# Moving the on-chip arena of matmul operands from 384 to 192 modulo 512 bytes

## What is computed

```python
for l in range(DEPTH):                                   # DEPTH = 1
    mod = (cond @ w_ada[l] + b_ada[l]).reshape(b_, N_SUB, 3, d)
    h = modulate(rms_norm(x, norm_gains[l, 0]), mod[:, 0, 0], mod[:, 0, 1])
    x = x + 0.5 * mod[:, 0, 2][:, None, :] * swiglu(h, ffn1_w_in[l], ffn1_w_down[l])
    h = modulate(rms_norm(x, norm_gains[l, 1]), mod[:, 1, 0], mod[:, 1, 1])
    proj = h @ w_in_mix[l]
...
    merged = (jax.nn.sigmoid(r_hg) * (y_hg @ w_up_hg[l])
              + jax.nn.sigmoid(r_gla) * (y_gla @ w_up_gla[l]))
    x = x + mod[:, 1, 2][:, None, :] * (merged @ w_out[l])
    h = modulate(rms_norm(x, norm_gains[l, 2]), mod[:, 2, 0], mod[:, 2, 1])
    x = x + 0.5 * mod[:, 2, 2][:, None, :] * swiglu(h, ffn2_w_in[l], ffn2_w_down[l])
return rms_norm(x, final_norm)
```

## Time and profile before

| | |
|---|---|
| median of 3 executions | 1189.76 us (1188.7 to 1189.96) |
| the profiled execution, its own time | 1188.77 us |
| its span, first to last instruction | 1186.9 us |
| TensorE busy | 1158.7 us, 98% |
| VectorE busy | 781.7 us, 66% |
| ScalarE busy | 507.5 us, 43% |
| GpSimd busy | 90.7 us, 8% |
| mean granted TensorE clock | 0.992 of full |

### The profile page before, as it was taken

How to read it: one execution, slowest core, us unless ns; L and a number is a source line. 1 busy time by engine, 2 the same in 40 slices (tenths; PEclk the granted TensorE clock), 3 DMA queues, 4 the chain that set the end, 5 groups by cost and what they waited for, 6 DMA issues and landing times.

```text
span 1186.9 us, 18541 instructions
## 1 busy us (share of the span) xinstructions
PE 1158.7 (98%) x7385; PEld 1039.3 (88%) x7385; DVE 781.7 (66%) x1061; ACT 507.5 (43%) x646; POOL 90.7 (8%) x137
## 2 busy tenths in 40 slices
PE   5999999999999999999999999999999999999997
PEld 5789999998889997877887888888999999998887
DVE  5788888767777677566463446755868887863222
ACT  6455554452222466555344322234455544452322
POOL 2000000002220122222010001000000000000000
PEclk8899999999999999999999999999999999999999
DMA  9433333337885131122221457442223333332211
GB/s 353 147 104 108 106 106 106 106 97 264 306 288 179 37 102 44 36 71 72 71 72 36 142 178 245 145 142 72 72 71 107 106 106 106 106 97 98 98 63 71
DMA packets 115126, 143.51 MB, mean 121 GB/s; under 512 B 4084, under 2 KB 102784, under 8 KB 115072
## 3 DMA queue, kind: packets, MB, share of 16 engines
q1 hardware_dynamic: 106800, 113.32, 29.2%
q0 software_dynamic: 8064, 29.36, 7.0%
q10 hardware_dynamic: 208, 0.08, 0.0%
HBM read 140.65 MB, written 2.10 MB: 120 GB/s over the span
## 4 chain that ended last, share of the span: by engine, by line
PE 87%; DVE 7%; ACT 4%; issue 1%; DMA 1%; SPq 0%; DVEq 0%; ACTq 0%
PE PS L819 29%; PE PS L575 16%; PE PS L577 15%; PE PS L576 15%; PE PS L898 1%; PE PS L934 1%; PE PS L620 1%; PE PS L904 1%; PE PS L621 1%; PE PS L622 1%; PE PS L733 1%; DVE ACC L1751 1%; DMA ADA<-in_w_ada_dram 1%; DVE ACC0a L1762 1%; ACT WH L1127 1%
## 5 line engine op out<-in xcount | busy, mean ns | idle before, releaser
L1649 DVE TENSOR_TENSOR WL<-RAW,WH 128x2048 fp32r<-128x2048 f32 (+2 forms) x55 | 120.5, 2191 | 129.4 <-ACT WH L1127 129.3
L575 PE MATMUL PS<-HH,WH 128*128 128x512 f32 (+2 forms) x488 | 186.1, 381 | 4.4 <-DVE HL L1677 3.0
L1127 ACT ACTIVATE WH<-RAW 128x2048 fp32r<-128x2048 f32 (+2 forms) x55 | 100.5, 1828 | 194.3 <-PE PS L577 187.7
L577 PE MATMUL PS<-HH,WL 128*128 128x512 f32 (+2 forms) x488 | 177.8, 364 | 0.0
L576 PE MATMUL PS<-HL,WH 128*128 128x512 f32 (+2 forms) x488 | 177.7, 364 | 0.0
L819 PE MATMUL PS<-HH,WH 128*128 128x256 f32 x576 | 163.3, 284 | 0.3
L819 PE MATMUL PS<-HL,WH 128*128 128x256 f32 x576 | 163.0, 283 | 0.0
L819 PE MATMUL PS<-HH,WL 128*128 128x256 f32 x576 | 163.0, 283 | 0.0
L575 PE MATMUL PS<-UH,WH 128*128 128x512 f32 (+1 forms) x416 | 147.0, 353 | 0.0
L577 PE MATMUL PS<-UH,WL 128*128 128x512 f32 (+1 forms) x416 | 145.8, 351 | 0.0
L576 PE MATMUL PS<-UL,WH 128*128 128x512 f32 (+1 forms) x416 | 145.8, 350 | 0.0
(11 more groups left out here) (320 smaller groups left out, 2244.3 us busy)
## 6 DMA issues: line engine op xcount, KB each, us to landing
RAW<-in_ffn_w_in_dram SPq DMA_DIRECT2D x42, 1024.0 KB, 5.1
ADAW<-in_w_ada_dram POOLq DMA_DIRECT2D x56, 512.0 KB, 5.6
RAW<-in_w_in_mix_dram SPq DMA_DIRECT2D x22, 1024.0 KB, 5.3
RAW<-in_ffn_w_down_dram SPq DMA_DIRECT2D x16, 1024.0 KB, 5.1
ADA<-in_w_ada_dram SPq DMA_DIRECT2D x16, 512.0 KB, 10.5
RAW<-in_ffn_w_down_dram SPq DMA_DIRECT2D x7, 768.0 KB, 4.5
RAW<-in_w_out_dram SPq DMA_DIRECT2D x3, 1024.0 KB, 5.1
XST<-in_x_dram SPq DMA_DIRECT2D x4, 512.0 KB, 5.3
```

Source lines behind the costliest of these rows:

```text
L575: mm(ps, whi, ahi, start=start, stop=False)
L577: return mm(ps, wlo, ahi, start=False, stop=stop)
L1127: A(WH[slot(n)][:, 0:size], RAW[slot(n)][:, 0:size], ACT.Copy).then_inc(unit_hi, 1)
L1649: V.tensor_tensor(WL[s][:, 0:size], RAW[s][:, 0:size], WH[s][:, 0:size].bitcast(F32), ALU.subtract)\
```

## The change

`MASKF` goes from a tensor of its own to an offset in the arena (86016), and the arena grows by 448 bytes, so that its content can begin anywhere in a window of 512 bytes. `arena_offset` then takes the first address at 192 modulo 512. The tensor `arena` now begins at 89472 (384 modulo 512, since `MASKF`'s 512 bytes are gone below it), and 320 bytes further, at 89792 = 175 x 512 + 192, its content. All that lies in the arena has moved by 192 bytes down. `RAW`, `WH`, `WL`, `X` stay where they were; the small tensors that came after `MASKF` have moved by a whole 512 bytes. Because `MASKF` now shares its bytes with rows that the feed-forward writes later, VectorE waits for the 27 steps of GpSimd ahead of its first product of gate and up values.

```diff
-        MASKF = sb("MASKF", [P, P])
...
-        arena = sb("arena", [P, (ARENA + 2 * H_BYTES) // 4])
+        arena = sb("arena", [P, (ARENA + 2 * H_BYTES) // 4 + 112])
...
+        MASKF = place("MASKF", [P, P], 86016)
...
+                if which == 0:
+                    dve.wait_ge(consts, 11 + 4 * len(LEVELS))
                 up_times_gate(which, 0, PS[:, 2:4, :], SG[:, :, :])
...
     size = arena.shape[1] * 4
-    return (nc.sbuf_base - size) // 32 * 32
+    start = (nc.sbuf_base - size) // 32 * 32
+    return start + (192 - start) % 512
```

## The result

Five executions of each kernel: 1183.1 us against 1188.7 us, ratio 0.9947 with a 95% interval of 0.9936 to 0.9958 (ratios below are given in the same way, the interval in brackets). The profiled execution of the changed kernel took 1181.76 us, its span is 1179.9 us, 7.0 us less than before.

The account below looks back on a forecast made before the run. TensorE was taken to bound the kernel, through its matmul pitch. All terms summed to 0 against the median of 1189.76 us, so 1189.8 us was forecast, with an 8-in-10 range of 1150 to 1200 us.

Parts of the forecast that it names:

- What bounds the kernel: Whole kernel: TensorE, busy 98% of the span, has next to no idle time in the large stages; only matmul pitch or new stops matter.
- The surplus of about 13 ns in each matmul: Full-clock matmul time that no column accounts for, hidden at half clock; over 6240 matmuls, 81 us at most to regain.
- Between them I take zero: Moving rows at 192 instead of 384: bounded by 81 us less and 42 us more, taken as no effect on pitch.
- The count of matmuls: 6240 matmuls at L819, 575 to 577 and 620 to 622 have moving operands in the arena; 384 do not.
- The control that I named: L620 to L622, moving rows staying at 128: if only L819 changes, the moving row's place is the cause; if both, the distance.
- The first rival: Arena matmuls: surplus depends on where a moving row begins; a quarter to half goes, 1169 to 1149 us; chance 0.38.
- The second rival: Same matmuls: rows starting off a multiple of 128 bytes deliver slower, up to 6.7 ns each, 1196 to 1232 us; chance 0.20.
- the forecast of no change: Whole kernel: no effect on the pitch, 1189.8 us, own range 1188 to 1191.5; chance 0.42.
- The small terms: Other arena operands at the start, 0.7 us either way, and VectorE's added wait, at most 0.1 us; both taken as zero.
- The wait on `consts`: VectorE's added wait for GpSimd's `MASKF` steps: already covered by 53 us, so between nothing and 0.1 us.
- the first load and the accumulations: Start of the kernel: 8.88 us load of modulation weights and 14.3 us of VectorE accumulations, taken as unchanged, 0.7 us either way.
- The formula that the prediction took from the Trainium skill's page: Matmul takes N / 1.2 ns at half clock, N / 2.4 + 2.5 ns at full; reaching it would save some 68 us, giving 1122.

## Why the prediction was wrong

**What bounds the kernel: right.** TensorE had no idle time to lose, and the gain is pitch, beside the 1.1 us of clock at the start of the profiled execution. **The surplus of about 13 ns in each matmul: right as the place to look.** It did shrink, by 2.3 ns at 256 columns, and by 6.5 ns in the first unit of `unit_v`; with 512 columns it grew by 1.7. That it is hidden at the half clock fits the 427 ns there at +64. That it is one figure for both widths does not hold: 512 columns less 256, from which it was worked out, is 107.7 ns at a distance of 0 and 116.2 at 32.

**The step that failed** is "Between them I take zero", with its reason: "neither the place of the moving row nor its distance from the stationary one shows in the pitch, for the three combinations that occur". The three combinations were +256, -256 and 0, and the runs show that the effect repeats every 256 bytes: I took three readings at one point for a flat line. The text said itself that the rows can't exclude an effect modulo 256, and then put most weight on them. In place of zero stand -10.0 us for 256 columns and +3.6 us for 512.

**The count of matmuls** was wrong in the same way: I took the 384 of `unit_v` out, since their moving rows stay, and left in the 168 with `LWH` and `LWL`, whose pitch did not change. Under the distance it is the other way round for both. The control that I named did its work: L620 changed along with L819, which the last part of the prediction reads as the distance.

**The first rival** had the right sign and, in its reason that rows "at 64 bytes past one another, instead of 256" may get in each other's way less, the right quantity, though its heading names the moving row's place. That "one nanosecond alone would give 1184" lies near the measured 1183.1 is luck, a sum of -2.3 ns and +1.7 ns; its likely sizes, a quarter to half of the surplus, were too large, because the two widths of matmul move against each other, which I did not consider. **The second rival** was wrong for 256 columns, and right for 512 in sign only: a unit of 128 bytes does not explain the runs, as the arena at 0 and at 256 is slower than at 384. The range held the time; the forecast of no change did not hold, since the interval of the ratio excludes it.

**The small terms: right.** The wait on `consts` and `MASKF` cost nothing that shows; the first load and the accumulations kept their durations to 0.1 us. What did differ at the start, 1.1 us, was the granted clock, and the kernel with the weights at 320 shows that the gain does not rest on it.

**The rules of the Trainium skill.** The page "SBUF — State Buffer" of the Trainium skill, section "Specifications (TRN2)", speaks of lines of 16 bytes, with a penalty for each new line; all places tried here are multiples of 32, so by that rule alone they should be equal. They are not: best and worst lie 1.4% apart. The page "TensorE: Matmul & The Clock Gate" of the Trainium skill, section "Step-by-step: what each phase is for", says that TensorE has two independent read ports, so that loading the next tile's weights takes no bandwidth from the running matmul. The measurement decides, and at the full clock it does not fit: the pitch follows the distance between what the two of them read. That the two reads get in each other's way is the likeliest reading, but where and how no run shows. The formula that the prediction took from the Trainium skill's page "TensorE: Matmul & The Clock Gate", section "Back-to-back issue gap", stands there for an isolated matmul; here, where each has its own load of weights, no distance brought the mean pitches under 117.0 and 227.6 ns.

## What to carry to other kernels

Where TensorE is busy all the time and its matmuls take longer at the full clock than half of what they take at the half clock (here 227 against 213 ns for 512 columns), try a few distances between the starts of the moving and the stationary rows, in steps of 32 bytes up to 256, and look at the pitch of each width of matmul by itself, stretch by stretch, since one distance can show two pitches; what is best for one width can be worst for another. Before taking a trace as a control, ask whether its cases differ in the quantity that could matter; equal readings at places that are equal in it tell nothing.

## What had not been expected of the hardware

- The pitch of fp32r matmuls, each with its own load of weights, depends on the distance of the two operands' starts modulo 256 bytes: 117.0 to 119.9 ns for 256 columns, 227.6 to 234.1 ns for 512. Moving both by the same amount changes nothing (119.94 and 227.64 ns against 119.94 and 227.67).
- The same instructions at the same distance can run in more than one rhythm: `unit_v` in the changed kernel kept 113.5 ns for one whole unit and 117.8 ns for most of a later one, and L819 and the 512 columns do the like (113.3 and 117.8 ns, 228.8 and 233.3 ns at +64, in the lines above). In both of those places the pitch differs before and after an interruption of the stream; that the interruption sets it was not tried. Perhaps because of the rhythms the times with the arena at 64 and at 320 spread more than elsewhere, 1185.2 to 1192.7 and 1180.7 to 1193.0 us in ten executions each.
- At the half clock the distance did not show: 427 ns for 512 columns at +64, 425.7 at 0.
